# Banded attention turns placed between the half units of the query and output projections

## The chip, the cores and the metric

One NeuronCore of a Trainium2 chip runs the whole program in one launch. The metric is the device time of that core in microseconds (us). Five engines work side by side and meet only at semaphores: PE (TensorE, matrix products into PSUM banks), DVE (VectorE), ACT (ScalarE), POOL (GpSimd), and SP, whose queue issues the DMAs that bring the weights. PEld is PE's weight load.

## The reference, cut to what matters

The program is two transformer blocks, on 512 tokens of width 1024. The change lies in the second layer of the first block. That layer does, with `h` the residual stream:

```
q   = partial_rope(rmsnorm(h) @ w_q)          # 16 heads of 64; k, v: 4 shared heads, made just before
s   = q k^T / 8, masked to a band             # blocks of 128 queries x 256 keys (the block before and its own)
m   = max(max(s), sink);  e = exp(s - m)
o   = (e / (sum(e) + exp(sink - m))) @ v      # the first block of queries has no block before: its 128 keys are masked
h   = h + o @ w_o
h   = h + relu(rmsnorm(h) @ w_up)^2 @ w_down  # the MLP
h   = h + sigmoid(rmsnorm(h) @ w_gate) * (p @ w_ple_proj)
```

The last product, `p @ w_ple_proj` (the PLE product), needs nothing of `h`.

## The kernel before, in words

Activations lie transposed in SBUF: 128 features on the partitions, 512 tokens along a row, 8 such tiles for the width of 1024. The precision is that of fp32, made of three faster products: each weight and each activation is split in a high part (`w_hi`, `x0h`, `x1h`) and a rest (`w_lo`, `x0l`, `x1l`), and each 128x128x512 product is three matmuls (hi x hi, hi x lo, lo x hi).

The weights are 289 units of 512 KB, in the order in which they are used; a unit is 8 blocks of 128x128, thus 24 matmuls. They go through a ring of 4 places. SP loads unit u+4 into its place when unit u is done (`unit_done`). ACT then makes `w_hi` (`act_split`, L195), and DVE `w_lo` (`dve_split`, L203), 3 units ahead of PE. `w_lo` lies over the loaded weights. A unit's result lies in one of four banks until DVE has taken it (`bank_free`).

The order of every engine's work is the order in which the code is written; there is no planner. Around the change the stages follow each other:

- `q_*`: 8 units of `w_q`. DVE scales each result (L1169) and rotates it (L1107, L1109, L1110) with one fp32 product of PE between (`ropeswap`, L1103).
- `att_*`: 16 turns, one for each of 4 key heads and 4 blocks of queries, 4 query heads in each. A turn has four scores products (PE L1234); mask and scale on the way out of PSUM (DVE L1269, twice), maximum (L1271), three tiny ones (L1275 to L1277); four exponentials with their sums (ACT L1311) and one of the sink (L1312); the reciprocal (DVE L1282, L1283) and the scaling of the weights (L1285); 8 transposes (PE L1243), two copies (ACT L1318), four products with v (PE L1254), and the split of the output in `x1h` (ACT L1322) and `x1l` (DVE L1289). The turns overlap each other: in step T, scores of turn T stand beside transposes of T-3 and outputs of T-4. POOL copies keys, queries and values for each key head first (L1216, L1217, L1219).
- `wo_*`: 8 units of `w_o`. DVE adds each result to `h` (L1337), ACT and DVE make the MLP's input of it (`act_x` L213, `dve_x` L218), and POOL squares it and adds it up for the norm (L232, L234).
- `p_*`: the PLE product, 2 units of weights with 4 products each, kept by ACT (L1003).
- `pe_norm` (L238): PE sums POOL's squares over the partitions. The MLP follows. The scale `R` is first needed when its first result is taken.

Of the kernel before, what the change touches and what calls it, by code (L numbers as in the profile page):

```python
# [47 lines left out]
U_KV, U_Q, U_O, U_P1, U_MLP1, U_GATE1 = 90, 94, 102, 110, 112, 176  # L48
# [44 lines left out]
def program(nc, a):  # L93
    ctx = ExitStack()
    with ctx:
# [801 lines left out]
        def mlp_parts(i, n, p_in, p_out, gain):  # L897
# [99 lines left out]
        def p_scalar(e, i):  # L997
            up = (U_P0, U_P1)[i]
            for j in range(2):
                act_split(e, up + j + AHEAD, 0)  # L1000
                for mm in range(4):
                    e.wait_ge(p_mm, 8 * i + 4 * j + mm + 1)
                    e.activation(Pp[:, 4 * j + mm], bk[4 + mm], ACT.Copy).then_inc(p_out, 1)  # L1003

        def p_vector(e, i):
            up = (U_P0, U_P1)[i]
            for j in range(2):
                dve_split(e, up + j + AHEAD, 0)
                e.wait_ge(unit_done, up + j + 1)
                e.sem_inc(bank_free, 1)  # L1010

        def p_tensor(e, i):
            up = (U_P0, U_P1)[i]
            e.wait_ge(p_ready, i + 1)
            for j in range(2):
                w = (up + j) % RING
                e.wait_ge(w_split, up + j + 1)
                for mm in range(4):
                    t = 8 * i + 4 * j + mm
                    if j:  # L1020
                        e.wait_ge(p_out, t - 3)
                    for k in range(2):
                        kk = 2 * mm + k
                        e.matmul(bk[4 + mm], w_hi[:, w, kk], p_h[:, k], start=(k == 0), stop=False)
                        e.matmul(bk[4 + mm], w_hi[:, w, kk], p_l[:, k], start=False, stop=False)
                        last = e.matmul(bk[4 + mm], w_lo[:, w, kk], p_h[:, k], start=False, stop=(k == 1))
                    last.then_inc(p_mm, 1)
                e.wait_ge(p_mm, 8 * i + 4 * j + 4)
                e.sem_inc(unit_done, 1)
            e.wait_ge(p_out, 8 * i + 5)  # L1030
# [58 lines left out]
        at = [x0_at]  # L1089
        Ks = own_buf("Ks", [2, LANES + TOK])  # L1090
        Qs = own_buf("Qs", [2, 2, TOK])
        Vs = own_buf("Vs", [2, 5, 64])
        Sm = own_buf("Sm", [4, 2, 2, 256])
        PT = put("PT", [LANES, 2, 512], at=acc_at)
        st = {n: own_buf("st_" + n, [4, 4]) for n in "mx nm df sm es rc".split()}
        assert at[0] <= x0_at + 32768
# [3 lines left out]
        def rope_tensor(e, u0, j, n4, src, turn):  # L1100
            e.wait_ge(bank_free, after(u0, j, n4, 5))
            e.wait_ge(rope_steps.sem, rope_steps.at("sin", (turn[0], turn[1] - 2)))
            e.matmul(bk[5 + j % 2], C("ropeswap"), src, start=True, stop=True).then_inc(rope_mm, 1)  # L1103

        def rope_vector(e, src, j, turn):

            rope_steps.next(e, turn).took("cos", e.tensor_tensor(one(t32[:, :]), src, one(C("rcos")), ALU.mult))  # L1107
            e.wait_ge(rope_mm, turn + 1 if isinstance(turn, int) else turn[0] + (turn[1] + 1))
            rope_steps.next(e, turn).took("sin", e.tensor_tensor(a32[:, :], bk[5 + j % 2], C("rsin"), ALU.mult))  # L1109
# [23 lines left out]
        def kv_vector(e):  # L1133
            rope_steps.open(e)
            for j in range(4):
# [5 lines left out]
                if j >= 2:  # L1141
                    e.wait_ge(bank_free, U_KV + j + 3)
                    rope_vector(e, kv32[:, j - 2:j - 1], j - 2, j - 2)
# [17 lines left out]
        def q_scalar(e):  # L1161
            turns(e, 8, lambda t, j: act_split(e, U_Q + j + AHEAD, t), once=lambda: v_keep(e))

        def q_vector(e):
            def body(t, j):
                dve_split(e, U_Q + j + AHEAD, t)
                m = t * 4 + j
                b = evac_start(e, U_Q, j, t)
                e.tensor_tensor(tile(q32, m), one(b), one(R[:, :]), ALU.mult).then_inc(bank_free, 1)  # L1169
                if j:  # L1170
                    e.wait_ge(bank_free, after(U_Q, j - 1, t, 5))
                    rope_vector(e, tile(q32, t * 4 + (j - 1)), j - 1, (t * 4, j + 1))
                if j == 3:
                    e.wait_ge(bank_free, after(U_Q, j, t, 5))
                    rope_vector(e, tile(q32, m), j, (t * 4, j + 2))
            turns(e, 8, body)

        def q_tensor(e):
            def body(t, j):
                pe_unit(e, U_Q, j, t, x0h, x0l, ready(x_ready, 32) if j == 0 else None)  # L1180
                m = t * 4 + j
                if j:
                    rope_tensor(e, U_Q, j - 1, t, tile(q32, t * 4 + (j - 1)), (t * 4, j + 1))
                if j == 3:
                    rope_tensor(e, U_Q, 3, t, tile(q32, m), (t * 4, j + 2))
            turns(e, 8, body, once=lambda: v_turn(e))

        att_copied = Steps(sem("att_copies"), "K Q V")
# [4 lines left out]
        att_turned = Steps(sem("att_turned"), "t0 t1", ahead=8)  # L1196
        att_kept = Steps(sem("att_weights"), "w0 w1", ahead=8)
# [3 lines left out]
        pads = sem("pads")  # L1201
        ATT_TURNS = 16

        def att_pool(e):
            att_copied.open(e)
            e.wait_ge(unit_done, U_O)
            for t, cut in ((Ks, Ks[:, :, 0:LANES]), (Vs, Vs[:, :, 0])):
                e.memset(cut, 0.0).then_inc(pads, 1)
            e.wait_ge(rope_steps.sem, rope_steps.at("sum", 9))
            e.wait_ge(k_dup, 8)  # L1210
            e.wait_ge(kv_tok, 2)
            with e.Fori(0, 2) as i:
                for x in range(2):
                    kh = (i * 2, x)
                    e.wait_ge(att_scored.sem, att_scored.at("s", (i * 8, 4 * x - 5)))
                    att_copied.next(e, kh).took("K", e.tensor_copy(Ks[:, x:x + 1, LANES:], tile(kdup, i * 2 + x)))  # L1216
                    att_copied.next(e, kh).took("Q", e.tensor_copy(Qs[:, x], q32[:, bass.ds(i * 4 + 2 * x, 2)]))  # L1217
                    e.wait_ge(att_outputs.sem, att_outputs.at("o", (i * 8, 4 * x - 5)))
                    att_copied.next(e, kh).took("V", e.tensor_copy(Vs[:, x, 1:5], v_tok[:, :, bass.ds(i * 128 + 64 * x, 64)]))  # L1219

        def att_tensor(e):
            for s in (att_scored, att_turned, att_outputs):
                s.open(e)
            e.wait_ge(pads, 2)

            def step(i, T):
                if runs(i, T, ATT_TURNS):
                    x, n, b = T // 4, T % 4, 2 * (T % 2)
                    if n == 0:
                        e.wait_ge(att_copied.sem, att_copied.at("Q", (i * 2, x)))  # L1230
                    e.wait_ge(att_maxima.sem, att_maxima.at("m1", (i * 8, T - 2)))
                    for g in range(4):
                        hf, gg = g % 2, g // 2
                        last = e.matmul(bank[b + hf][:, gg * 256:gg * 256 + 256], Qs[64 * hf:64 * hf + 64, x, gg, n * LANES:(n + 1) * LANES],  # L1234
                                        Ks[64 * hf:64 * hf + 64, x, n * LANES:(n + 2) * LANES], start=True, stop=True)
                    att_scored.took("s", last)
                q = T - 3
                if runs(i, q, ATT_TURNS):
                    e.wait_ge(att_scales.sem, att_scales.at("scale", (i * 8, q)))
                    for kt in range(2):  # L1240
                        e.wait_ge(att_kept.sem, att_kept.at(f"w{kt}", (i * 8, q - 1)))
                        for g in range(4):
                            last = e.transpose(bank[5 + kt][:, g * LANES:(g + 1) * LANES], Sm[:, q % 4, g // 2, g % 2, kt * LANES:(kt + 1) * LANES], C("ident"))  # L1243
                        att_turned.took(f"t{kt}", last)
                q = T - 4
                if runs(i, q, ATT_TURNS):
                    x, n = q % 8 // 4, q % 4
                    if n == 0:
                        e.wait_ge(att_copied.sem, att_copied.at("V", (i * 2, q // 4)))
                    e.wait_ge(att_kept.sem, att_kept.at("w1", (i * 8, q)))  # L1250
# [1362 lines left out]
```

## Time and profile before

| | |
|---|---|
| runs, us | 2079.78, 2080.70, 2086.28; median 2080.7 |
| profiled execution, us | 2082.57 |
| its span, us | 2080.8 |
| PE busy | 1947.3 us (94%) |
| DVE busy | 1268.3 us (61%) |
| ACT busy | 900.5 us (43%) |
| POOL busy | 430.1 us (21%) |
| mean granted clock of PE | 0.975 of full speed |

A matmul counts as busy from its start to its modelled end, though the next one starts before that end; so the distance between starts, not the mean of one, says what a stream of matmuls takes. The page cuts the span into 40 slices of 52 us. PE is 90% busy or more in nearly all of them; the slices from 728 to 832 us show 60 to 70%, and next to no DMA.

### The profile page before, as it was taken

What the parts mean: (1) busy time and instruction counts of PE and PEld (TensorE: products, weight loads), DVE (VectorE), ACT (ScalarE), POOL (GpSimd) and SP (SyncE); (2) the same over time, 40 slices, a digit from 0 to 9 for tenths busy, and PEclk for the clock granted to TensorE, in tenths of its full rate; (3) what the DMA queues carried; (4) which work ended last, traced back from release to release, by engine and by line L of the source; (5) the groups of instructions that cost most, each with busy time, mean ns of one, the idle gap of its engine ahead of it and who ended that gap; (6) DMA issues with size and microseconds to landing.
All of it is one profiled execution on the core that took longest, in us unless ns stands there. A gap on an engine that the chain in (4) does not pass through costs nothing.

```text
span 2080.8 us, 27316 instructions
## 1 busy us (share of the span) xinstructions
PE 1947.3 (94%) x9494; PEld 1565.4 (75%) x9494; DVE 1268.3 (61%) x1783; ACT 900.5 (43%) x1507; POOL 430.1 (21%) x295
## 2 busy tenths in 40 slices
PE   3889999999999967999999999999999998999996
PEld 1668788888887745788888887878878886777774
DVE  7873443343469587543343468987667765777764
ACT  3674432232334255432332333445445552366661
POOL 5672200000043010300000043342212224000003
PEclk8899999999999979999999999999999999999998
DMA  4113332333332200333333332222222222212221
GB/s 178 44 34 111 91 101 91 101 92 100 95 98 90 83 1 11 92 101 93 98 97 95 101 91 81 82 61 67 66 81 64 69 72 62 90 61 63 69 72 61
DMA packets 54522, 166.98 MB, mean 80 GB/s; under 512 B 13216, under 2 KB 13344, under 8 KB 53920
## 3 DMA queue, kind: packets, MB, share of 16 engines
q1 hardware_dynamic: 54432, 165.78, 26.6%
q8 instruction: 56, 0.92, 0.2%
q14 instruction: 34, 0.28, 0.0%
HBM read 161.30 MB, written 2.10 MB: 79 GB/s over the span
## 4 chain that ended last, share of the span: by engine, by line
PE 76%; DVE 9%; ACT 5%; POOL 3%; issue 2%; DMA 2%; DVEq 0%; POOLq 0%; SPq 0%; PEldq 0%; ACTq 0%
PE bank L183 15%; PE bank L184 15%; PE bank L185 15%; PE bank L1501 4%; PE bank L1502 4%; PE bank L1503 4%; PE bank L2107 2%; DMA raw<-in_w_dram 2%; PE bank L2109 2%; PE bank L2108 2%; PE bank L1516 1%; POOL acc L234 1%; PE bank L1517 1%; PE bank L1518 1%; ACT w_hi L195 1%
## 5 line engine op out<-in xcount | busy, mean ns | idle before, releaser
L203 DVE TENSOR_TENSOR w_lo<-raw,w_hi 128x1024 fp32r<-128x1024 f32 x286 | 366.8, 1282 | 466.2 <-ACT w_hi L195 465.0
L195 ACT ACTIVATE w_hi<-raw 128x1024 fp32r<-128x1024 f32 x289 | 305.8, 1058 | 627.3 <-DMA raw<-in_w_dram 627.2
L183 PE MATMUL bank<-x1h,w_hi 128*128 128x512 f32 x744 | 291.6, 392 | 6.5 <-DVE x1l L218 6.5
L185 PE MATMUL bank<-x1h,w_lo 128*128 128x512 f32 x744 | 289.8, 389 | 0.0
L184 PE MATMUL bank<-x1l,w_hi 128*128 128x512 f32 x744 | 289.7, 389 | 0.0
L183 PE MATMUL bank<-x0h,w_hi 128*128 128x512 f32 x704 | 277.9, 395 | 0.0
L185 PE MATMUL bank<-x0h,w_lo 128*128 128x512 f32 x704 | 274.1, 389 | 0.0
L184 PE MATMUL bank<-x0l,w_hi 128*128 128x512 f32 x704 | 274.0, 389 | 0.0
L232 POOL TENSOR_TENSOR sq<-h 128x512 f32 (+1 forms) x64 | 79.0, 1234 | 783.2 <-DVEq L940 659.7
L183 PEld LDWEIGHTS bank<-x1h,w_hi 128*128 128x128 f32 x744 | 139.7, 188 | 38.0 <-DVE x1l L218 7.8
L184 PEld LDWEIGHTS bank<-x1l,w_hi 128*128 128x128 f32 x744 | 139.8, 188 | 29.3 <-issue 0.7
L185 PEld LDWEIGHTS bank<-x1h,w_lo 128*128 128x128 f32 x744 | 139.8, 188 | 29.1
L1501 PE MATMUL bank<-x1h,w_hi 128*128 128x512 f32 x384 | 156.0, 406 | 0.0
L183 PEld LDWEIGHTS bank<-x0h,w_hi 128*128 128x128 f32 x704 | 132.1, 188 | 29.8 <-issue 2.5
L184 PEld LDWEIGHTS bank<-x0l,w_hi 128*128 128x128 f32 x704 | 132.1, 188 | 29.3 <-issue 2.3
L185 PEld LDWEIGHTS bank<-x0h,w_lo 128*128 128x128 f32 x704 | 132.1, 188 | 27.5
L1502 PE MATMUL bank<-x1l,w_hi 128*128 128x512 f32 x384 | 151.1, 394 | 0.0
L1503 PE MATMUL bank<-x1h,w_lo 128*128 128x512 f32 x384 | 150.9, 393 | 0.0
L234 POOL TENSOR_TENSOR acc<-acc,sq 128x512 f32<-128x512 f32 x64 | 103.3, 1614 | 5.0
L919 DVE TENSOR_TENSOR x1l<-a,x1h 128x512 f32 x64 | 44.3, 693 | 92.7 <-ACT a L909 92.7
L907 ACT ACTIVATE x1h<-t 128x512 f32 x64 | 40.5, 632 | 130.7 <-DVE t L917 130.7
L1501 PEld LDWEIGHTS bank<-x1h,w_hi 128*128 128x128 f32 x384 | 73.0, 190 | 17.9 <-issue 1.9
(382 smaller groups left out, 3457.3 us busy)
## 6 DMA issues: line engine op xcount, KB each, us to landing
raw<-in_w_dram SPq DMA_DIRECT2D x289, 512.0 KB, 3.6
h<-in_xT_dram SPq DMA_DIRECT2D x1, 2048.0 KB, 13.0
Ur<-in_xu_dram SPq DMA_DIRECT2D x8, 256.0 KB, 2.7
out_dram<-h SPq DMA_DIRECT2D x8, 256.0 KB, 2.2
const<-in_const_dram SPq DMA_DIRECT2D x1, 1028.0 KB, 13.9
B_st<-in_B_dram SPq DMA_DIRECT2D x1, 1024.0 KB, 7.7
C_st<-in_C_dram SPq DMA_DIRECT2D x1, 1024.0 KB, 15.1
p_in<-in_pT_dram SPq DMA_DIRECT2D x1, 1024.0 KB, 4.8
```

What stands on the lines that cost most here:

```text
L183: e.matmul(b, w_hi[:, w, k], xh[:, k], start=(k == 0), stop=False)
L184: e.matmul(b, w_hi[:, w, k], xl[:, k], start=False, stop=False)
L185: last = e.matmul(b, w_lo[:, w, k], xh[:, k], start=False, stop=(k == KT - 1))
L195: e.activation(w_hi[:, z], raw[:, z], ACT.Copy).then_inc(hi_split, 1)
L203: e.tensor_tensor(w_lo[:, z], raw[:, z], w_hi[:, z].bitcast(F32), ALU.subtract).then_inc(w_split, 1)
L232: e.tensor_tensor(one(sq[:, :]), tile(h, m), tile(h, m), ALU.mult).then_inc(squared, 1)
L234: e.tensor_tensor(acc[:, :], acc[:, :], sq[:, :], ALU.add).then_inc(acc_ready, 1)
L919: e.tensor_tensor(tile(x1l, m), one(a32[:, :]), tile(x1h, m).bitcast(F32), ALU.subtract).then_inc(a_ready, 1)
L1501: e.matmul(b, w_hi[:, w, k], x1h[:, k], start=(k == 0), stop=False)
L1502: e.matmul(b, w_hi[:, w, k], x1l[:, k], start=False, stop=False)
L1503: last = e.matmul(b, w_lo[:, w, k], x1h[:, k], start=False, stop=(k == KT - 1))
L2107: e.matmul(b, w_hi[:, w, k], xh[:, k], start=(k == 0), stop=False)
```

## The change

- The stages `q_*`, `att_*` and `wo_*` and the PLE product of this layer become one window, `win_*`, of 18 places of one unit each: 8 of `w_q`, 4 of the first half of `w_o`, 2 of the PLE product, 4 of the second half of `w_o`. Each is cut in two half units of 12 matmuls, so there are 36 positions p = 0 to 35.
- `w_o` is cut by rows: the first four units use only the heads 0 to 7 for all 8 output tiles, and the last four the heads 8 to 15. Each half unit makes one output tile's half sum, and DVE adds it to `h`, so there are 16 such additions in place of 8. The two banks 0 and 1 (2 and 3 for the last unit) take the results in turn.
- Turn T of attention has its scores at position T+5, its exponentials at T+6, scaling and transposes at T+7, products with v at T+8 and the rest at T+8 and T+9. PE's order within a position is: half unit, rotation product, products with v, transposes, scores. There is now one pair of banks for the scores (2 and 3), not two, so that scores of T+1 wait for DVE's reading of T.
- The copies by POOL are gone: PE reads `kdup`, `q32` and `v_tok` themselves. In every fourth turn (first block of queries) the 128 masked keys are left out everywhere.
- The PLE product uses two banks in place of four. It no longer stands between the last unit of `w_o` and `pe_norm`.

```diff
+        Q_SLOTS, O_AT, P_AT, WIN_SLOTS = 8, (8, 14), 12, 18
+        FIRST_TURN, ATT_TURNS = 5, 16
+        def p_bank(t):
+            return bk[4 + t % 4] if t < 8 else bk[2 + t % 2]
+        def o_acc(part, i, o):
+            return bk[(2 if part and i == 3 else 0) + o]
+        def win_tensor(e):
+            for p in range(2 * WIN_SLOTS):
+                n, half = p // 2, p % 2
+                win_half(e, n, half)
...
+                if half == 0 and 1 <= n <= Q_SLOTS:
+                    e.wait_ge(bank_free, win_evacuated(n - 1))
+                    e.matmul(q_bank(n - 1), C("ropeswap"), q32[:, n - 1], start=True, stop=True).then_inc(rope_mm, 1)
+                T = turn_at(p - 3)
...
+                    e.wait_ge(att_kept.sem, att_kept.at("w", T))
...
+                T = turn_at(p - 2)
+                if T is not None:
+                    e.wait_ge(att_scales.sem, att_scales.at("scale", T))
...
+                T = turn_at(p)
...
+                    e.wait_ge(att_maxima.sem, att_maxima.at("m1", T - 1))
...
+            e.wait_ge(wo_half_free, 7)
...
+                else:
+                    e.wait_ge(wo_half_free, 4 * part + i)
...
-            att_pool(e)
...
-            q_tensor(e)
-            att_tensor(e)
-            wo_tensor(e)
+            win_tensor(e)
...
-    cols(w_o[0], 8)
+    pairs(w_o[0], 0)
     ple(w_ple_proj[1])
+    pairs(w_o[0], 1)
```

PE, in the middle of attention. `Ks`, `Qs` are keys and queries, `Sm` the weights, `PT` their transposes, `Vs` the values; each row is one group. Before:

```order
1364 L1243 MATMUL bank<-const,Sm 128x128 x8
1365 L1254 MATMUL bank<-PT,Vs 64x256 x4
1366 L1234 MATMUL bank<-Ks,Qs 128x256 x4
1367 L1243 MATMUL bank<-const,Sm 128x128 x8
1368 L1254 MATMUL bank<-PT,Vs 64x256 x4
1369 L1234 MATMUL bank<-Ks,Qs 128x256 x4
```

PE, in position 14 of the window: the end of its half unit, then (L1267) the rotation product of the unit before, and one group each of three turns. After:

```order
1368 L1219 MATMUL bank<-x0h,w_hi 128x512
1369 L1220 MATMUL bank<-x0l,w_hi 128x512
1370 L1221 MATMUL bank<-x0h,w_lo 128x512
1371 L1267 MATMUL bank<-q_124,const 128x512
1372 L1278 MATMUL bank<-PT,v_tok 64x256 x4
1373 L1287 MATMUL bank<-const,Sm_135 128x128 x8
1374 L1298 MATMUL bank<-kdup,q_124 128x256 x4
1375 L1219 MATMUL bank<-x0h,w_hi 128x512
1376 L1220 MATMUL bank<-x0l,w_hi 128x512
```

The same groups stand between half units, and the products with v have moved ahead of the transposes.

DVE, one whole step of attention before:

```order
537 L1269 SCALAR_TENSOR_TENSOR Sm<-bank,const 128x512 x2
538 L1271 TENSOR_REDUCE st_mx<-Sm 128x4
539 L1275 TENSOR_TENSOR st_mx<-st_mx,par 128x4
540 L1276 TENSOR_SCALAR st_nm<-st_mx 128x4
541 L1277 TENSOR_TENSOR st_df<-par,st_mx 128x4
542 L1282 TENSOR_TENSOR st_rc<-st_sm,st_es 128x4
543 L1283 RECIPROCAL st_rc<-st_rc 128x4
544 L1285 TENSOR_TENSOR Sm<-Sm,st_rc 128x1024
545 L1289 TENSOR_TENSOR x1l<-bank,x1h 128x2x128
```

DVE, one position with a rotation in it after, up to the next wait for scores (L1363). `q` is the query projection, `t` a temporary:

```order
522 L1319 TENSOR_TENSOR st_rc<-st_sm,st_es 128x4
523 L1320 RECIPROCAL st_rc<-st_rc 128x4
524 L1322 TENSOR_TENSOR Sm_127<-Sm_127,st_rc 128x1024
525 L1326 TENSOR_TENSOR q_124<-bank,R 128x512
526 L1108 TENSOR_TENSOR t_63<-q_124,const 128x512
527 L1346 TENSOR_TENSOR x1l<-bank,x1h 128x2x128
528 L203 TENSOR_TENSOR w_lo<-raw,w_hi 128x1024
529 L1363 SCALAR_TENSOR_TENSOR Sm_135<-bank,const 128x512 x2
530 L1365 TENSOR_REDUCE st_mx<-Sm_135 128x4
```

The scaling of q, a part of its rotation and the weight split now stand between a turn's scaling and the next turn's scores.

PE, at the end of the window. Before, a PLE product stood ahead of the norm's product (L238):

```order
1556 L1024 MATMUL bank<-p_h,w_hi 128x512
1557 L1025 MATMUL bank<-p_l,w_hi 128x512
1558 L1026 MATMUL bank<-p_h,w_lo 128x512
1559 L238 MATMUL bank<-acc,const 128x512
1560 L970 UNCONDITIONAL_BRANCH
```

After, the last half unit of `w_o` stands there:

```order
1648 L1241 MATMUL bank<-x1h,w_hi 128x512
1649 L1242 MATMUL bank<-x1l,w_hi 128x512
1650 L1243 MATMUL bank<-x1h,w_lo 128x512
1651 L238 MATMUL bank<-acc,const 128x512
1652 L973 UNCONDITIONAL_BRANCH
```

The 48 PLE matmuls that stood between `w_o` and the norm are now ahead of the last four units of `w_o`.

## Rows read from the trace of the kernel before

**Rows 1.** Busy time by stage: stretch, its length, PE, PEld, DVE, ACT, POOL, PEclk, DMA, GB/s

```profile
673.00:727.00 54.00, 53.16 (x219) 39.93 (x217) 31.04 (x41) 14.50 (x17) 0.45 (x2) 1.00 0.28 82
727.00:732.00 5.00, 0.00 (x0) 0.00 (x0) 2.66 (x4) 0.00 (x0) 1.64 (x2) 0.88 0.15 61
732.00:764.00 32.00, 22.23 (x120) 14.79 (x120) 27.67 (x58) 18.28 (x66) 4.14 (x7) 0.70 0.00 1
764.00:821.00 57.00, 39.84 (x265) 24.80 (x266) 49.62 (x102) 36.72 (x127) 2.49 (x4) 0.91 0.00 1
821.00:865.00 44.00, 44.00 (x195) 36.39 (x195) 23.56 (x24) 14.64 (x17) 19.25 (x15) 1.00 0.28 84
```

**Rows 2.** Waits of PE in 735 to 815: total, times, longest

```profile
PE bank L1243 <- DVE Sm L1285: 23.0, 13, 5.8
```

**Rows 3.** Timeline of one attention turn: start, duration, what [idle before]

```profile
776.07 1.09 PE L1243 MATMUL bank<-const,Sm 128*128 128x128 f32 x8 [0.18 <-DVE Sm L1285]
776.27 1.28 DVE L1269 SCALAR_TENSOR_TENSOR Sm<-bank,const 128x512 f32<-128x512 f32 x2
...
777.09 1.09 PE L1254 MATMUL bank<-PT,Vs 128*64 128x256 f32 x8
...
778.11 1.13 PE L1234 MATMUL bank<-Ks,Qs 64*128 64x256 f32 x8
...
779.32 0.16 DVE L1282 TENSOR_TENSOR st_rc<-st_sm,st_es 128x4 f32<-128x4 f32 x1
...
780.87 0.42 DVE L1289 TENSOR_TENSOR x1l<-bank,x1h 128x256 fp32r<-128x256 f32 x1
...
781.20 1.28 DVE L1269 SCALAR_TENSOR_TENSOR Sm<-bank,const 128x512 f32<-128x512 f32 x2
```

**Rows 4.** Timeline around two units of the query projection and its first one

```profile
673.46 0.80 PE L183 MATMUL bank<-x0h,w_hi 128*128 128x512 f32 x1
...
718.50 0.69 DVE L1169 TENSOR_TENSOR q<-bank,R 128x512 f32 x1 [0.51 <-PE bank L185]
...
722.16 1.06 ACT L195 ACTIVATE w_hi<-raw 128x1024 fp32r<-128x1024 f32 x1 [5.42 <-DMA raw<-in_w_dram]
...
724.29 0.40 PE L185 MATMUL bank<-x0h,w_lo 128*128 128x512 f32 x1
...
724.84 0.69 DVE L1169 TENSOR_TENSOR q<-bank,R 128x512 f32 x1 [0.36 <-PE bank L185]
```

**Rows 5.** Timeline from the last output unit to the norm

```profile
864.39 0.39 PE L1024 MATMUL bank<-p_h,w_hi 128*128 128x512 f32 x1
...
868.47 1.06 ACT L195 ACTIVATE w_hi<-raw 128x1024 fp32r<-128x1024 f32 x1 [1.89 <-DMA raw<-in_w_dram]
869.43 2.04 ACT L1003 ACTIVATE Pp<-bank 128x512 f32<-128x512 f32 x4
...
876.59 1.10 PE L238 MATMUL bank<-acc,const 128*128 128x512 f32 x2 [0.30 <-ACT Pp L1003]
```

**Rows 6.** Timeline of POOL and DVE where they meet, and where they don't

```profile
628.22 1.62 POOL L234 TENSOR_TENSOR acc<-acc,sq 128x512 f32<-128x512 f32 x1
628.61 1.78 DVE L1059 TENSOR_TENSOR a<-gs,Pp 128x512 f32<-128x512 f32 x1
...
650.32 0.68 DVE L1059 TENSOR_TENSOR a<-gs,Pp 128x512 f32<-128x512 f32 x1
...
838.92 1.04 POOL L232 TENSOR_TENSOR sq<-h 128x512 f32 x1 [2.81 <-DVEq L1339]
840.04 1.62 POOL L234 TENSOR_TENSOR acc<-acc,sq 128x512 f32<-128x512 f32 x1
```

**Rows 7.** Stage table around an idle stretch of PE elsewhere

```profile
1734.00:1738.00 4.00, 0.00 (x0) 0.00 (x0) 2.36 (x3) 3.16 (x4) 2.49 (x2) 0.97 0.30 118
1738.00:1742.00 4.00, 2.65 (x6) 2.17 (x7) 2.83 (x4) 0.00 (x0) 0.00 (x0) 0.50 0.00 0
1742.00:1746.00 4.00, 4.00 (x14) 3.14 (x13) 0.00 (x0) 0.00 (x0) 0.00 (x0) 0.68 0.00 0
```

More of the change, by code:

```diff
@@ L1200, in program @@
         att_lo = Steps(sem("att_out_lo"), "lo", ahead=8)
[L1201 to L1219, printed above, removed]
@@ L1236, in step @@
                     att_scored.took("s", last)
[L1237 to L1250, printed above, removed]
-                    e.wait_ge(att_lo.sem, att_lo.at("lo", (i * 8, q - 2)))
-                    for hf in range(2):
-                        for kt in range(2):
-                            last = e.matmul(bank[7 - 3 * (q % 2)][64 * hf:64 * hf + 64, 0:256], Vs[:, x, n + kt], PT[:, kt, hf * 256:hf * 256 + 256], start=(kt == 0), stop=(kt == 1))
-                    att_outputs.took("o", last)
@@ L1301, in att_scalar, with win_scalar @@
+        def win_scalar(e):
             for s in (att_exps, att_kept, att_hi):
                 s.open(e)
-            def step(i, T):
-                q = T - 1
-                if runs(i, q, ATT_TURNS):
-                    z = q % 4
-                    e.wait_ge(att_maxima.sem, att_maxima.at("dif", (i * 8, q)))
+            for p in range(2 * WIN_SLOTS + 1):
+                n, half = p // 2, p % 2
+                T = turn_at(p - 1)
+                if T is not None:
+                    z, k0 = T % 4, keys(T)
+                    e.wait_ge(att_maxima.sem, att_maxima.at("dif", T))
@@ L1332, in wo_vector @@
-        def wo_vector(e):
-            def body(t, j):
-                dve_split(e, U_O + j + AHEAD, t)
-                m = t * 4 + j
-                b = evac_start(e, U_O, j, t)
-                e.tensor_tensor(tile(h, m), tile(h, m), one(b), ALU.add).then_inc(bank_free, 1)
-                e.wait_ge(bank_free, after(U_O, j, t, 5))
-                e.sem_inc(h_ready, 1)
-                dve_x(e, 5, m, "mlp1", x0h, x0l)
-            turns(e, 8, body, late=lambda: p_split_vector(e, 1))
-        def wo_tensor(e):
-            def there(k):
-                return att_lo.sem, att_lo.at("lo", 4 * (k // 2) + 3)
-            turns(e, 8, lambda t, j: pe_unit(e, U_O, j, t, x1h, x1l, there if j == 0 else None))
+                if half == 0 and n < WIN_SLOTS:
+                    act_split(e, U_Q + n + AHEAD, 0)
@@ L2505, in cols, with pairs @@
             unit(w, r0, c0 + 128 * m)
+    def pairs(w, pair):
+        w = w[pair * 512:pair * 512 + 512].reshape(4, 128, 4, 2, 128)
+        for j in range(4):
+            units.append(w[:, :, j].transpose(1, 2, 0, 3).reshape(128, KT, 128))
     def ple(w):
```

361 lines of the change are left out of this document (220 added, 141 removed).

## The prediction

> **What bounds the kernel now.** I read the page's slices first, then the table by stage, then the waits and the timeline of one turn. PE is the bound nearly everywhere. Two stretches differ [rows 1]: 727 to 732, where PE does nothing, and 732 to 821, where PE's overlapping records cover 62 of 89 us. There DVE is busy 77.3 of 89 us, and 49.6 of 57 from 764 on. PE's waits in that stage name DVE's scaling of the weights [rows 2]. One turn shows the same [rows 3]: DVE starts the masks at 776.27 and again at 781.20, so a turn takes 4.93 us, and DVE has no gap in it. PE's three groups start at 776.07, 777.09 and 778.11, some 3.1 us of work, and then PE waits. So 16 turns with start and end cost the 94 us from 727 to 821 [rows 1], of which PE has about 50 us of work at full clock (16x3.1).
>
> The stretch that the change rewrites runs from the first product with `w_q`, at 673.5, to the norm's product, at 876.6 [rows 4, 5]. That is **203.1 us** before.
>
> **Is it hidden?** The total of PE's work in the new window is easily summed. Twelve matmuls at the distance of 0.2265 us of the stream (24 of them and one rotation product of 0.87 give the 6.34 us from 718.50 to 724.84 [rows 4]) are 2.72 us a half unit, and 32 of these are 87. The rotations add 7, the PLE products 11.2, v's transposes 1, and attention 43 (3.06 for each of 12 full turns, about 1.6 for each of 4 short ones). That is 149 us, and 54 us could go. But DVE's work doesn't shrink, and PE and DVE now wait for each other once in each position. So I add up the chain, not the work.
>
> Call S the moment at which the scores of a position are ready. Durations are those of rows 3 and 4:
>
> - DVE: masks 1.31, maximum 1.25, three tiny ones 0.5: 3.06 from 776.27 to 779.32 with no gap. Then reciprocal and scaling of the turn before, 1.55 (779.32 to 780.87). So scaled weights are there at S+4.7.
> - An even position with a rotation: DVE takes q next, 0.61 and 0.1 to be seen, at S+5.45. PE's half unit ended at S+2.7 and its rotation product waits for that. Behind it are queued products with v, transposes and scores: 0.87+3x1.02. The period is **9.4 us**, of which PE waits 2.7.
> - An odd position: PE waits with the transposes for S+4.75, then 2x1.02 and 0.13: **6.9 us**. DVE has as much of its own: 4.6, half of the rotation 1.45, rest of the output 0.36, new masks.
>
> The short turns have no row. The nearest are the 512 and the 256 elements of DVE, 0.68 and 0.42. I take 0.75 for the masks, 0.65 for the maximum, 0.6 for scaling, and half for PE and ACT. Then every cycle of four positions is 8.2 + 5.8 + 8.9 + 6.85 us. Were the cut worth nothing, the window would be 12 us longer; that is the upper bound, and I take the lower, since time follows size in the two rows.
>
> | positions | us |
> |---|---|
> | 0 to 4: five halves 13.6, two rotations 1.7, v's transposes 1.0, one wait of 0.7 | 17.0 |
> | 5, first scores behind the rotation's sum | 4.05 |
> | 6, 7: pipeline fills | 11.6 |
> | 8 to 16: 3x8.9 + 2x8.2 + 2x6.85 + 2x5.8 | 68.4 |
> | 17: its half unit writes the bank of the last rotation, and waits for DVE to read it: 5.5+2.72+2x1.02+0.6 | 10.9 |
> | 18 to 20: 5.8 + 5.85 + 7.2 (DVE also splits `p`) | 18.9 |
> | 21 to 23: last turns | 15.1 |
> | 24 to 27: PLE | 16.2 |
> | 28 to 35: last four units | 26.4 |
> | wait for the norm | 8.0 |
> | sum | **196.5** |
>
> The last three need words. **PLE:** with two banks the third product waits until ACT has kept the first. ACT's queue has the split of a weight unit in front of that, and this waits for a DMA. From the end of a unit to ACT's start took 3.7 to 4 us (864.3 to 868.47 [rows 5]; 718.2 to 722.16 [rows 4]). So PE waits about 2 us in each unit, beside 11.2 of work and 0.7 at the ends. Before, four banks hid the same thing but for 0.3 us at each end.
>
> **Last four units:** bank 0 is written by every unit's first half, and only DVE's addition frees it. DVE's queue has in front of it the weight split, which waits for ACT, which waits for the DMA: 3.95+1.05+1.2, then `x0l` 0.7 and the addition 0.7 behind the end of the unit before. That is 7.6 and more, against 5.44: about 1.2 us in each unit and 0.2 for the second bank. 4x5.44 + 4.6 = 26.4.
>
> **Norm:** before, 12.2 us of PLE product (864.4 to 876.6) covered POOL's last squares. Now nothing does. POOL's two operations for a tile take 2.66 plus 0.1 [rows 6], and tiles come every 3 to 4 us. Rows 6 also show that POOL and DVE block each other: DVE's product of two SBUF tensors took 1.78 us where it began inside POOL's addition, 0.68 where POOL was idle. DVE has the split and two `x0l` in each unit. POOL's 2x2.45 (what is left of 2.66 once blocked parts go) and DVE's 2.4 make 7.3 us a unit, more than the 6.6 in which tiles come. POOL thus ends some 8 us behind PE: 3.7 for DVE's last addition and the last tile, the rest in arrears. Without any blocking it would be about 6, with full blocking and dearer additions 9.5.
>
> The Trainium skill (SBUF — State Buffer, section SBUF: two separate sides) says that VectorE and GpSimd share one pair of ports under an exclusive lock that the first holds for its whole instruction. The trace agrees: 0.39 us after POOL's start, DVE's operation lasted until 0.55 us behind POOL's end.
>
> **Clock.** After a stretch in which PE was idle (1734 to 1738), the granted clock was 0.50 and 0.68 for the next 8 us [rows 7]: 4x0.5+4x0.32 = 3.3 us lost, part of it still idle. The wait for the norm is 8 us long, so I add **2.2** (bounds 0 and 3.3). In exchange the half clock of the old attention stage (0.70 from 732 to 764) goes; it cost little there, as DVE set the pace.
>
> So 196.5+2.2 = 198.7 against 203.1: **4.4 us less**. The profiled execution took 2082.57 (span 2080.8 and 1.8 around it), 1.9 above the median of 2080.7; the same span with 4.4 less is 2078.2, and against the median of the runs it is **2076.3**, say 2076.
>
> Costed at nothing: POOL's copies (PE's idle stretch from 727 to 732, which goes with them, is inside the 94); the eight further additions to `h` (0.61 each, in positions 17 to 24 beside PE's chain, in the end inside the 26.4); the changed order of weights (same bytes); the missing loops. ACT was busy for 55 us in the old stage's 89 [rows 1], 3.4 a turn; with half a weight split that is 4 us in a position, beside 5.8 or more.
>
> **Rivals.**
>
> *A. The waits overlap better than my chain* (DVE's reading released earlier, fewer serial steps). For it: PE's work is only 149 us. Against: every link of the chain stands in one queue behind the other. If half of the 27 us that I count as waits for DVE in positions 6 to 17 went, the time would be 2063.
>
> *B. Slower: PE's clock falls inside the window.* Place: positions 6 to 23, where PE waits 1.5 to 2.7 us in each. In the old stage it had 0.70 and 0.91 [rows 1] with waits of much that size. At half clock a position takes 11 us for 6.9 and 13.5 for 9.4, about 4.1 more; over 16 positions 66 us. The share at which it decides is 7%: then the 4.4 us are gone. At one fifth, 13 us, the time is 2089. Against it: PE will be at work for 75 to 80% of the time there, against 62 of 89 with smaller products, and half units at the full array stand between.
>
> The Trainium skill (TensorE: Matmul & The Clock Gate, section A second HAM failure mode: psum-queue depth-cycling) says that short idle times between groups of matmuls can make the clock swing. The trace agrees for the old stage, with 0.70 and 0.91; whether it holds with the half units in between, no row shows.
>
> *C. The steps between engines are dearer than the rows.* Each position has five waits of PE that were not there. At 0.1 us more in each, over 36 positions, 4 us: the change brings nothing, 2080.
>
> *D. The change hides nothing of attention.* Then only short turns and POOL's copies count, with the end's 8 us against them: also about 2080. It would need positions of 8.7 us on average from 6 to 23, against my 6.9.
>
> **Chances.** Forecast 0.38, of which half lies beyond 0.3% (6.2 us, about what a measurement of this kernel can tell) and half within. A 0.23. B 0.21. C and D together 0.18. So faster 0.19+0.23 = 0.42, same 0.19+0.18 = 0.37, slower 0.21. The forecast's own range is 2070 to 2081. The range to hold 8 in 10 goes down to A with half of its gain and half again as much, 2062, and up to B's 2089 and a little, 2090.
>
> **What would show it.** Right: in the new profile from the first `w_q` product to L238 some 198 us; a distance of 9 us between the scores (L1298) of an odd and the next even position, and under 7 for the other; PE's longest single wait at L238, 6 to 10 us, released by POOL; two waits of 2 us at the PLE products for ACT. Wrong: a granted clock under 0.95 over the window (B), distances of 8 and 6 (A), or 10 and 8 (C); a wait at L238 under 4 us, if POOL keeps up. The rest of the program must take the same time, but for a shift.

## The result and the profile after

| | before | after |
|---|---|---|
| runs, us | 2082.15 median of 7 (2077.93 to 2086.28) | 2094.4 median of 7 (2091.95 to 2100.59) |
| ratio, 95% interval | | 1.0069 [1.0051, 1.0086] |
| span of the profiled execution, us | 2080.8 | 2092.6 |
| PE busy, us | 1947.3 (94%) | 1947.2 (93%) |
| mean granted clock | 0.975 | 0.976 |
| first product with `w_q` to L238, us | 203.1 | 209.9 (670.16 to 880.02) |

The changed kernel is slower by 12 us by the medians (14 by the ratio), and the forecast of 2076 was wrong, in sign too. PE's busy time is the same to 0.1 us, which doesn't say where the time went: a wait is not busy, a slow clock makes the same work longer, and the short turns took work away. So I read the rewritten stretch by stages, which answers to [rows 1]. Columns: stretch, length, PE, PEld, DVE, ACT, POOL, granted clock, DMA share, GB/s.

```profile
691.00:764.00 73.00, 60.36 (x330) 39.76 (x332) 58.97 (x118) 34.77 (x115) 0.00 (x0) 1.00 0.13 40
764.00:778.00 14.00, 9.14 (x36) 5.35 (x34) 7.98 (x15) 4.59 (x17) 0.00 (x0) 0.76 0.05 20
778.00:792.00 14.00, 8.52 (x38) 5.73 (x34) 6.80 (x13) 3.50 (x12) 0.00 (x0) 0.76 0.08 17
792.00:811.00 19.00, 17.18 (x102) 11.92 (x104) 17.19 (x35) 11.72 (x37) 0.00 (x0) 1.00 0.14 45
811.00:827.00 16.00, 14.66 (x85) 10.33 (x84) 11.98 (x21) 7.51 (x21) 0.00 (x0) 1.00 0.12 34
827.00:844.00 17.00, 13.14 (x48) 9.19 (x47) 2.87 (x3) 6.18 (x11) 0.00 (x0) 0.92 0.20 62
844.00:872.00 28.00, 23.23 (x96) 17.83 (x96) 14.78 (x15) 8.88 (x11) 17.49 (x13) 0.99 0.24 76
872.00:880.00 8.00, 0.00 (x0) 0.01 (x1) 5.06 (x6) 2.79 (x4) 5.25 (x4) 0.71 0.21 66
880.00:887.00 7.00, 6.98 (x17) 4.88 (x18) 3.71 (x2) 1.63 (x2) 0.53 (x1) 0.60 0.00 0
```

Attention no longer leaves PE at 62 of 89 us: through 691 to 764 PE is busy for 60.4 of 73 us at full clock. The stretches that stand out are two of 14 us from 764 to 792, with the clock at 0.76, and the 8 us from 872 to 880, where PE does nothing, with 0.60 behind them. PE's waits from 673 to 900 (what waits, the releaser, total us, times, longest) name all three places:

```profile
PE bank L238 <- POOL acc L234: 8.7, 1, 8.7
PE bank L1287 <- DVE Sm L1322: 7.7, 8, 2.3
PE bank L1267 <- DVE q L1326: 7.6, 4, 2.4
PE bank L1241 <- DVE a L1113: 5.5, 1, 5.5
PE bank L1241 <- DVE x1l L1346: 4.9, 1, 4.9
PE bank L1013 <- ACT Pp L1005: 3.5, 2, 2.1
PE bank L1241 <- DVE h L1336: 3.4, 2, 2.7
```

The 23.0 us for the scaled weights [rows 2] are now 7.7. In their place stand four waits for q's reading (L1267), one for a rotation (L1113), one for the norm, and the wait for `x1l`, 4.9 us, which my table didn't have. Its place in the timeline, position 16, the first half unit of `w_o`:

```profile
764.84 1.29 DVE L1363 SCALAR_TENSOR_TENSOR Sm<-bank,const 128x512 f32<-128x512 f32 x2 [0.16 <-PE bank L1298]
...
768.30 1.22 DVE L1322 TENSOR_TENSOR Sm<-Sm,st_rc 128x1024 f32<-128x1024 f32 x1
769.44 0.68 DVE L1326 TENSOR_TENSOR q<-bank,R 128x512 f32<-128x512 f32 x1
770.16 0.69 DVE L1108 TENSOR_TENSOR t<-q,const 128x512 f32<-128x512 f32 x1
770.77 0.42 DVE L1346 TENSOR_TENSOR x1l<-bank,x1h 128x256 fp32r<-128x256 f32 x1
...
771.24 0.80 PE L1241 MATMUL bank<-x1h,w_hi 128*128 128x512 f32 x1 [4.86 <-DVE x1l L1346]
771.84 0.63 PE L1242 MATMUL bank<-x1l,w_hi 128*128 128x512 f32 x1
...
784.31 0.77 PE L1241 MATMUL bank<-x1h,w_hi 128*128 128x512 f32 x1 [5.48 <-DVE a L1113]
```

PE stops in the middle of the half unit: it needs the output of turn 7 (heads 4 to 7), and DVE makes the low part of that output only behind this position's masks, scaling, q and cosine. The matmuls behind it show the clock: 0.63 us for 0.39, and starts 0.43 us apart for 0.23. The clock had already fallen inside the wait: it was at half from 769.6 to 776.4, while the wait ended at 771.2. The end, which answers to [rows 5] and [rows 6]:

```profile
870.39 1.06 ACT L195 ACTIVATE w_hi<-raw 128x1024 fp32r<-128x1024 f32 x1 [4.29 <-DMA raw<-in_w_dram]
871.48 1.23 DVE L203 TENSOR_TENSOR w_lo<-raw,w_hi 128x1024 fp32r<-128x1024 f32 x1 [3.29 <-ACT w_hi L195]
...
873.29 0.68 DVE L1336 TENSOR_TENSOR h<-h,bank 128x512 f32<-128x512 f32 x1
874.28 1.04 POOL L232 TENSOR_TENSOR sq<-h 128x512 f32 x1 [2.95 <-DVEq L1339]
875.40 1.59 POOL L234 TENSOR_TENSOR acc<-acc,sq 128x512 f32<-128x512 f32 x1
877.17 1.04 POOL L232 TENSOR_TENSOR sq<-h 128x512 f32 x1 [0.18 <-POOL acc L234]
878.29 1.59 POOL L234 TENSOR_TENSOR acc<-acc,sq 128x512 f32<-128x512 f32 x1
```

L238 starts behind the last of these, at 880.02, after 8.74 us of wait. POOL was not behind when this wait began. It stood idle for 2.95 us until DVE had added the seventh tile to `h` (873.29), and DVE's queue had a weight split ahead of that addition, which waited for ACT, which waited for a DMA. The rest, 5.6 us, is POOL's work for the last two tiles.

### The profile page after: what moved, and what is told of

The parts are those of the page before. It is cut to its first block, busy times and chain, and to the rows that moved or that the text cites. A ratio compares the mean times of both kernels' runs of the same rounds, so it can differ in the third digit from the quotient of the medians.

```text
span 2092.6 us, 27161 instructions
## 1 busy us (share of the span) xinstructions
PE 1947.2 (93%) x9462; PEld 1557.9 (74%) x9462; DVE 1263.3 (60%) x1791; ACT 896.9 (43%) x1503; POOL 421.9 (20%) x281
## 4 chain that ended last, share of the span: by engine, by line
PE 74%; DVE 10%; ACT 6%; DMA 3%; issue 3%; POOL 2%; DVEq 0%; POOLq 0%; SPq 0%; PEldq 0%
PE bank L183 14%; PE bank L185 13%; PE bank L184 13%; PE bank L1561 4%; PE bank L1563 3%; PE bank L1562 3%; DMA raw<-in_w_dram 3%; PE bank L2167 2%; PE bank L2169 2%; PE bank L2168 2%; PE bank L1576 1%; ACT w_hi L195 1%; PE bank L1577 1%; PE bank L1578 1%; DVE w_lo L203 1%
## 5 line engine op out<-in xcount | busy, mean ns | idle before, releaser
L183 PE MATMUL bank<-x1h,w_hi 128*128 128x512 f32 x680 | 266.6, 392 | 6.4 <-DVE x1l L218 6.4
L185 PE MATMUL bank<-x1h,w_lo 128*128 128x512 f32 x680 | 264.9, 390 | 0.0
L184 PE MATMUL bank<-x1l,w_hi 128*128 128x512 f32 x680 | 264.8, 389 | 0.0
L183 PE MATMUL bank<-x0h,w_hi 128*128 128x512 f32 x640 | 251.6, 393 | 0.0
L184 PE MATMUL bank<-x0l,w_hi 128*128 128x512 f32 x640 | 249.7, 390 | 0.0
L185 PE MATMUL bank<-x0h,w_lo 128*128 128x512 f32 x640 | 249.7, 390 | 0.0
L1561 PE MATMUL bank<-x1h,w_hi 128*128 128x512 f32 x384 | 156.6, 408 | 0.0
L1563 PE MATMUL bank<-x1h,w_lo 128*128 128x512 f32 x384 | 151.8, 395 | 0.0
L1562 PE MATMUL bank<-x1l,w_hi 128*128 128x512 f32 x384 | 151.8, 395 | 0.0
L184 PEld LDWEIGHTS bank<-x1l,w_hi 128*128 128x128 f32 x680 | 127.8, 188 | 27.0 <-issue 0.7
L185 PEld LDWEIGHTS bank<-x1h,w_lo 128*128 128x128 f32 x680 | 127.8, 188 | 26.6
L184 PEld LDWEIGHTS bank<-x0l,w_hi 128*128 128x128 f32 x640 | 120.6, 188 | 26.2 <-issue 1.2
L185 PEld LDWEIGHTS bank<-x0h,w_lo 128*128 128x128 f32 x640 | 120.6, 188 | 25.2
```

The lines of the kernel that those rows point to most:

```text
L183: e.matmul(b, w_hi[:, w, k], xh[:, k], start=(k == 0), stop=False)
L184: e.matmul(b, w_hi[:, w, k], xl[:, k], start=False, stop=False)
L185: last = e.matmul(b, w_lo[:, w, k], xh[:, k], start=False, stop=(k == KT - 1))
L1561: e.matmul(b, w_hi[:, w, k], x1h[:, k], start=(k == 0), stop=False)
L1562: e.matmul(b, w_hi[:, w, k], x1l[:, k], start=False, stop=False)
L1563: last = e.matmul(b, w_lo[:, w, k], x1h[:, k], start=False, stop=(k == KT - 1))
```

## The experiments

Theories. **T1**: the wait for turn 7 and the clock behind the two 5 us waits make the miss. **T2**: positions are dearer than the chain throughout, so the interleaving doesn't pay. **T3**: the end (PLE ahead, norm bare) makes it. Each run stands as its ratio to runs of before on its own chip, whose medians were 2080.1 to 2081.9. "Window" is the stretch from the first `w_q` product to L238 in the profiled execution; in after it is 209.9, and the distances between scores are 9.2, 7.3, 8.1 and 6.0 in a cycle of four, 14.0 in position 16 and 14.2 in 17.

**1. No wait for turn 7.** The first half unit reads heads 0 to 3 twice; the second takes the wait.

```diff
+                    early = n == O_AT[0] and half == 0
-                        e.wait_ge(att_lo.sem, att_lo.at("lo", 8 * part + 4 * (k // 2) + 3))
-                    x = 4 * part + k
+                        e.wait_ge(att_lo.sem, att_lo.at("lo", 3 if early else 8 * part + 4 * (k // 2) + 3))
+                    x = 4 * part + (k % 2 if early else k)
```

> Changes part of the computation: the first half unit of the output projection (position 16) reads the head tiles 0 and 1 twice, in place of 2 and 3, so that it need not wait for turn 7's output, which DVE makes in the same position. All else as in the changed kernel. Theory 1 (the missed wait and the clock that falls behind it): the 4.86 us wait goes, position 16 takes 9 us in place of 14.0 from scores to scores, no half clock begins there; 5 us less in the window, 210 to 205, and if the next wait (position 17, 5.5 us) alone is too short to lower the clock, 3 more. Rival 2 (every position is dearer than counted, the waits only show it): the wait moves to the next position, window 208 or more.

Measured: 2087.5, ratio 1.0028 [1.0011, 1.0046]. Position 16 takes 9.2 for 14.0. Position 17 takes 13.1; in its stretch the clock is still down. The window is 207.8, 2.1 less where I expected 5: two ordinary positions took 1.6 and 0.5 more than in after, since the clock fell there too, and it fell once more in the last four units (at 856.4). That is not rival 2, since the wait of position 17 did not grow (5.4 us for 5.5).

```profile
764.00:778.00 14.00, 9.13 (x54) 5.47 (x48) 11.84 (x21) 7.43 (x24) 0.00 (x0) 1.00 0.14 39
778.00:792.00 14.00, 10.67 (x54) 7.86 (x56) 7.94 (x20) 4.90 (x19) 0.00 (x0) 0.76 0.11 37
```

So this wait is a cause, 4.8 us with its clock, and it is not the whole of the 12.

**2. Matmuls into both waits.** 18 and 17 products of 128x512 into banks that are overwritten before they are read; the waits for DVE stay.

```diff
+                if n == O_AT[0] and half:
+                    e.wait_ge(att_kept.sem, att_kept.at("w", 9))
+                    filler(e, 17, w, bk[4])
...
+                if n == O_AT[0] and half == 0:
+                    e.wait_ge(att_lo.sem, att_lo.at("lo", 3))
+                    filler(e, 18, w, bk[0])
```

> Adds 18 matmuls of 128x128x512 ahead of the half unit of position 16 and 17 ahead of that of position 17, into banks that are free then; their results are overwritten, and the output is the same. They fill some 4 us of each of the two waits, which end when they did. Theory 1 (the clock falls because PE idles for 5 us): no half clock from 760 to 800; the positions take 11.3 and 10.9 us in place of 14.0 and 14.2, window 6 us shorter, 204. Rival 2 (the clock falls for another reason, as the small products of attention): the half clock stays, and the window is as long or longer (18 matmuls at half clock are 7.7 us).

Measured: 2085.0, ratio 1.0008 [0.9991, 1.0024]. Positions 16 and 17 take 11.6 each. The window is 207.2, 2.7 less, where I expected 204; the profiled execution, 2092.1 us, was the second longest of its ten.

```profile
694.00:704.00 10.00, 8.63 (x37) 6.17 (x38) 7.11 (x14) 2.72 (x11) 0.00 (x0) 0.83 0.16 53
...
710.00:716.00 6.00, 3.55 (x11) 1.47 (x11) 5.49 (x10) 3.12 (x10) 0.00 (x0) 0.84 0.00 0
...
770.00:782.00 12.00, 11.21 (x56) 7.80 (x56) 8.45 (x16) 4.98 (x19) 0.00 (x0) 1.00 0.10 38
782.00:794.00 12.00, 10.68 (x61) 7.66 (x59) 6.80 (x13) 4.05 (x13) 0.00 (x0) 1.00 0.11 31
```

More work for PE made the kernel faster, so the clock behind the waits costs by itself: 28.2 - 23.2 = 5.0 us in the two positions. The first two rows show the same execution with a lower clock in two ordinary places where after had 1.00. Such falls come and go between executions, and the medians of this section contain them.

**3. Matmuls ahead of the norm.** 68 products of 128x256 into a free half of a bank.

```diff
+        def filler(e, count, w):
+            for _ in range(count):
+                e.matmul(bank[6][:, 256:512], w_hi[:, w, 0], x1h[:, 0, 0:256], start=True, stop=True)
...
+            filler(e, 68, 3)
```

> Adds 68 matmuls of 128x128x256 ahead of the norm's product, into a bank that is free; output the same. They fill 7.7 of the 8.7 us in which PE waits for POOL. Theory 1: the wait's end doesn't move, the clock stays full behind it, and from the norm's product to the third result of the MLP it takes 18 us as before the change, not 20.5: 2.5 us less in all. Rival 2 (what comes behind the norm is late for DVE's or ACT's sake): nothing changes there.

Measured: 2090.4, ratio 1.0032 [1.0015, 1.0049]; window 209.7. L238 now takes 1.10 us for 2.04, and behind it the clock stays up:

```profile
870.00:878.00 8.00, 8.00 (x68) 7.84 (x66) 5.48 (x6) 3.17 (x4) 5.00 (x4) 1.00 0.22 66
878.00:886.00 8.00, 7.58 (x33) 5.93 (x32) 5.18 (x3) 1.63 (x2) 0.84 (x2) 1.00 0.01 2
```

From L238 to the third result of the MLP it takes 17.9 us for 20.5, so the clock behind the norm costs 2.6 us in the profiles; I had 2.2. The medians differ by 4.0, with intervals that nearly touch.

**4. PLE product last**, with its four banks, in the interleaved order.

```diff
-            return bk[4 + t % 4] if t < 8 else bk[2 + t % 2]
+            return bk[4 + t % 4]
-        Q_SLOTS, O_AT, P_AT, WIN_SLOTS = 8, (8, 14), 12, 18
+        Q_SLOTS, O_AT, P_AT, WIN_SLOTS = 8, (8, 12), 16, 18
...
-                    e.wait_ge(p_out, t - 1)
+                    e.wait_ge(p_out, t - 3)
```

> Undoes one part: the PLE product stands again behind the last unit of the output projection, with four banks. Theory 1: PE's wait of 8.7 us at the norm goes, and the two waits of 2 us for ACT at the PLE products shrink to 0.3; the third cost, bank 0 waiting for DVE in the last four units, stays; the clock behind the norm stays full (2.6). In all 12 to 14 us less, window 197, the total equal to the kernel before or slightly under. Rival 2 (POOL is so far behind that the 12 us of PLE don't cover it, or the second half of the output projection now waits for turn 15's output): 5 us less at most.

Measured: 2075.4, ratio 0.9966 [0.9947, 0.9986]; window 195.7, 14.2 less, and no half clock behind the norm.

```profile
PE bank L1241 <- DVE a L1113: 5.5, 1, 5.5
PE bank L1241 <- DVE x1l L1347: 4.9, 1, 4.9
PE bank L1241 <- DVE h L1337: 2.7, 1, 2.7
...
PE bank L238 <- ACT Pp L1005: 0.3, 1, 0.3
PE bank L1013 <- ACT Pp L1005: 0.3, 1, 0.3
```

The largest single cost of the change is the PLE product's new place, together with its two banks for four, which this run doesn't separate: 19 us by the medians. T3 holds as a price. But my sum had 12.0 of the 14.2 us of window.

**5. Four banks for the last units**, so that PE need not wait for DVE's additions.

```diff
-            return bk[(2 if part and i == 3 else 0) + o]
+            return bk[(2 if part and i % 2 else 0) + o]
...
```

> One change against the changed kernel: the last four units of the output projection go over four banks in place of two. Same output. Theory 1: PE's waits for DVE's additions there (3.4 us in all) go, and so does most of the gap between the units; but the norm's product still waits for POOL, which gets each tile only when DVE comes to it; so PE just waits longer at the norm (8.7 to 11) and the window is within 1 us of 209.9. Rival 2 (the banks hold the whole tail back): window 3 us shorter or more.

Measured: 2091.8, ratio 1.0048 [1.0031, 1.0065], not told apart from after. Window 212.0, of which two ordinary positions have a lower clock. The waits for additions are gone, and the norm's took their place:

```profile
PE bank L238 <- POOL acc L234: 12.1, 1, 12.1
PE bank L1013 <- ACT Pp L1005: 2.8, 1, 2.8
```

PE reached the norm earlier and L238 came no sooner. Here POOL does run behind: its last four tiles follow each other with 0.18 us between tiles, up to 882.8, where in after it stood idle for 2.95 us and then had two tiles left. So with the end as it is, DVE's and POOL's queues set L238, and a faster PE only waits longer.

**6. DVE takes q first.** In even positions DVE reads the bank of `w_q` (L1326) ahead of the reciprocal and the scaling, not behind them. Same instructions, other order.

```diff
+                m = n - 1
+                if half == 0 and 0 <= m < Q_SLOTS:
+                    e.wait_ge(unit_done, U_Q + m + 1)
+                    e.tensor_tensor(q32[:, m], q_bank(m), R[:, :], ALU.mult).then_inc(bank_free, 1)
```

> One change of order on DVE against the changed kernel: in even positions it takes q out of its bank before the scaling of the turn before, not behind it. Same instructions. Theory 1 (a chain through one queue sets the length of a position): the rotation product starts 1.5 us earlier, PE then waits for the scaling for a part of that; even positions take 8 us in place of 9.2, others are unchanged; window 5 to 6 us shorter, 204. Rival 2 (DVE is simply full and order doesn't matter): no position changes by more than 0.3 us.

Measured: 2084.4, ratio 1.0025 [1.0015, 1.0034]; window 203.1, 6.8 less. Positions of 9.2 take 7.6, those of 8.1 take 6.6. The four waits of 7.6 us in all become two:

```profile
PE bank L1241 <- DVE a L1113: 5.5, 1, 5.5
PE bank L1241 <- DVE x1l L1347: 4.7, 1, 4.7
...
PE bank L1267 <- DVE q L1318: 1.8, 2, 0.9
```

**7. The joint reordered.** In position 16 DVE makes turn 7's low part first, in position 17 the last rotation first.

```diff
+                if p == 16:
+                    rest()
+                if p == 17:
+                    rope_sin(e, q32[:, 7:8], q_bank(7), 9)
```

> Two changes of order on DVE, in positions 16 and 17 alone: turn 7's output (for which PE waits 4.9 us) is made ahead of the scaling in 16, and the last rotation (5.5 us of wait) ahead of it in 17. Theory 1: the waits shrink to 2 and 4 us and the positions to 11.5 and 10.5 with a full clock, 12 to 13 if one half clock remains; window 4 to 9 us shorter. Rival 2 (the clock falls for the attention products): waits shrink, but half clock stays at 770 to 795 and the gain is under 4 us.

Measured: 2090.5 of four runs, ratio 1.0055 [1.0034, 1.0075], unclear by the runs. In the trace the window is 204.3; the positions take 10.6 and 11.6, with waits of 2.0 and 3.9 us, and at each the clock is down for less long:

```profile
763.50:774.50 11.00, 9.01 (x38) 4.87 (x38) 8.45 (x16) 5.08 (x19) 0.00 (x0) 0.84 0.10 39
774.50:786.00 11.50, 7.56 (x38) 5.27 (x36) 6.80 (x13) 3.51 (x13) 0.00 (x0) 0.85 0.10 19
```

Two slow stretches of 3.4 us where after had two of 6.8.

**8. The kernel before with short turns and direct reads alone**: no POOL copies, 128 masked keys left out of every fourth turn, no interleaving. The turns are written out in place of a loop, as in after.

```diff
+        def keys(T):
+            return 128 if T % 4 == 0 else 0
...
-            att_pool(e)
```

> The kernel before, with one part of the change alone: no copies by POOL (PE reads keys, queries and values themselves) and 128 keys in place of 256 in every fourth turn. Nothing is interleaved. Theory 1 (the interleaving itself, with the waits it makes, costs more than it hides): DVE sets the pace of the old stage, 4.93 us a turn; four turns lose 1.7 each, 6.9, and the start loses its 4.4 us for the copies. 11 us less than the kernel before, 2071, so that of the changed kernel's result the interleaving has cost some 20. Rival 2 (the short turns save little, for DVE's fixed costs): 5 us less at most, 2077.

Measured: 2074.5, ratio 0.9969 [0.9957, 0.9980]; window 193.1, 10 less than before's, where I expected 11. The medians differ by only 6 where I expected 10. A short turn's operations took 0.76, 0.69 and 0.69 us on DVE, where I had put 0.75, 0.65 and 0.6.

**9. Full turns in the window.** The first block of queries attends to 256 keys, the first 128 repeated; its result is another one.

```diff
-            return 128 if T % 4 == 0 else 0
+            return 0
```

> The changed kernel without the short turns: every fourth turn reads 256 keys as the others do (for the first block of queries those of blocks 0 and 1 under the ordinary mask, so its result is another). Theory 1: 12 us more by my chain (8.2 becomes 9.4 and so on), window 222; the interleaving by itself then stands at 2106 against 2081, and what held the changed kernel near the one before was the part that has nothing to do with interleaving. Rival 2 (positions are bound by PE's own work): 6 us more at most.

Measured: 2105.9, ratio 1.0113 [1.0087, 1.0139]; window 221.3, 11.4 more than after.

**10. All repairs** (4, 5, 6 and 7 together). Edit: the lines of those four.

> The changed kernel with all repairs: PLE product last, on four banks; four banks for the last four units of the output projection; q taken first in even positions; the two changes of order in 16 and 17. Same computation. Theory 1: from the window of 195.7 us with PLE last, 5.6 go for the even positions, 4 to 9 for positions 16 and 17, 3 for the banks: 178 to 183, total 2058 to 2063, under the kernel before by 1%. Rival 2 (the savings overlap, since each only moves PE's wait to the next link): 190 or more, 2070.

Measured: 2062.2, ratio 0.9904 [0.9890, 0.9919]; window 181.9. Positions 16 and 17 take 11.0 and 11.6, with waits of 2.6 and 3.9 us and a granted clock of 0.84 and 0.85 over them.

**11. All repairs, and 8 and 11 matmuls into the two waits that are left.**

```diff
+                    filler(e, 11, w, bk[4])
...
+                    filler(e, 8, w, bk[0])
```

> The kernel with all repairs, and 8 and 11 further matmuls of 128x128x512 in the two waits that are left in positions 16 and 17 (2.6 and 3.9 us); their results are overwritten. Theory 1: in the repaired kernel's profile two half clocks of 3.4 us lie there, and these positions took 11.0 and 11.6 us; with the clock held they take 9.5 to 10.5 each, 2 to 3 us less in all, total 2059. Rival 2 (the waits are too short to matter to the clock): no change, 2062.

Measured: 2054.7, ratio 0.9871 [0.9849, 0.9893]; window 176.9. Positions 16 and 17 take 9.4 and 10.0, 3.2 us less. The medians differ by 7.5 where I expected 2 to 3; in this profile the clock never falls in the window, where run 10's had one more fall, at an ordinary position (709.3).

```profile
670.00:765.00 95.00, 86.71 (x443) 59.14 (x443) 76.90 (x147) 47.05 (x139) 0.00 (x0) 1.00 0.17 51
765.00:786.00 21.00, 19.86 (x115) 13.99 (x111) 15.88 (x30) 9.98 (x29) 0.00 (x0) 1.00 0.09 26
786.00:847.00 61.00, 55.92 (x274) 42.36 (x274) 46.07 (x63) 29.44 (x63) 24.70 (x17) 1.00 0.23 69
```

This version beats both kernels, before by 1.3%; 0.3% of that is what run 8 had without interleaving.

## Why the prediction was wrong, step by step

The window was to be 196.5 and was 209.9. By places in after:

| step | predicted | measured |
|---|---|---|
| to the scores of position 7 | 32.65 | 32.4 |
| positions 8 to 15 | 59.5 | 61.1 |
| position 16 | 8.9 | 14.0 |
| position 17 | 10.9 | 14.2 |
| 18 to 20 | 18.9 | 18.9 |
| 21 to 27 | 31.3 | 33.1 |
| last four units | 26.4 | 27.4 |
| wait for the norm | 8.0 | 8.7 |
| clock behind it | 2.2 | 2.6 |

- **The step that failed** has two parts, both in positions 16 and 17: a wait that my sum left out, 2.7 us, and the clock of long waits inside the window, which I put at nothing, 5.0 us. The first is the row "8 to 16: 3x8.9 + ...": I priced position 16 as one more even position. Its half unit is the first of `w_o`, and its second half reads heads 4 to 7. The wait for `w_o`'s operand stood nowhere in my sum; I had followed banks and rotations only. At full clock it costs 11.6 - 8.9 = 2.7 (run 2), and 9.2 without it (run 1) shows that 8.9 was right for the rest.
- **The clock in the window.** Rival B named it and put it in the wrong place. It asked for 7% of positions 6 to 23 at half clock, through waits of 1.5 to 2.7 us. In after the ordinary positions from 691 to 764, with such waits, had 1.00. The falls came in the two waits of about 5 us, lasted 6.8 us each, and cost 5.0 us in all (run 2) where rival B charged 4.1 for each position hit. I had position 17's wait right, 5.5 for 5.48, and gave it no clock, although I had charged the norm's wait 2.2. The two positions are 8.4 of the 13.4 us: 3.4 from waits, 5.0 from the clock. T1 thus explains most of the miss in the window, not all. The Trainium skill (TensorE: Matmul & The Clock Gate, section A second HAM failure mode: psum-queue depth-cycling) says that frequent short idle times between groups of matmuls can make the clock swing. Some executions agree at ordinary positions, with half clock for 3.4 us at 702.8 and 740.3 in run 1; the two falls of after are another case, each at one long wait.
- **The chain per position** was right in its kind: T2 explains only 1.6 us over eight positions. That is rival C at a fifth of a microsecond each. Part of it is my distance of the stream: (6.34 - 0.87)/24 is 0.228, not 0.2265, which is 0.02 us a half unit.
- **The end** was near in size: PE's waits for ACT at the PLE product are 1.4 and 2.1 us (I had 2 and 2), the norm's wait 8.7 for 8.0, released by POOL. But its working does not give the 8.0: 7.3 for 6.6 us a unit is 2.8 over four units, and with 3.7 makes 6.5. Nor were there such arrears, since POOL stood idle for 2.95 us before its last two tiles; what I left out is DVE's weight split, which waited for the DMA ahead of the seventh tile. The 8.0 was partly luck. In the last four units 7.6 against 5.44 is 2.2 us a unit, where I wrote 1.2; measured are 27.4 for 26.4 in all. The PLE row's parts add up to 15.9, not 16.2. Run 4 puts the PLE's move at 14.2 us of window. My terms for it were 16.2 - 12.2 for the product and 8.0 for the norm, 12.0 in all; most of the rest are the 1.8 us too few in 21 to 27, where the clock was at half from 841.3 to 844.7, a fall that I hadn't charged.
- **What the sum compares with.** Before to after is a chain of three steps. Short turns and direct reads: 203.1 to 193.1 (run 8). Interleaving with the PLE last: 193.1 to 195.7. The PLE's move: 195.7 to 209.9. In ratios 0.9969, 0.9966 and 1.0069, so the middle step is nothing that the runs can tell. So the interleaving in this order, net of its own waits, brings nothing, which is what rival D said. Its 8.7 us a position does not belong to its 2080: 18 positions of 8.7 are 32 us more than my chain, and 2080 needs 4. From the scores of position 5 at 690.99 to the PLE's first product at 826.81 are 7.5 for each of 18, where I had 6.9, and that was enough. With the changes of runs 5 to 7 added (run 10) the interleaving does pay: 193.1 becomes 181.9, and 0.9969 becomes 0.9904. Without the move of the PLE my sum stood at 184.5, and 195.7 was measured.
- **Chances.** Slower had 0.21, by B alone. D with the end at my own terms (12.0 and 2.2 of clock, where I wrote 8) would have stood at 2086, 5.5 above before, just inside what I counted as the same.

From the profiled windows +6.8 and the clock +2.6 make 9.4 of the 12.2 us between the medians. The other 2.8 stay open. Outside the window the two profiles differ by 3.3 us less ahead of it and 5.8 more behind, and neither need be a cost of the change: from L238 to the end, the same code as in after took 1204.6 us in run 1 and 1206.0 in run 5, against 1212.6 in after and 1204.2 in before.

## What to carry over

When units with different operands are lined up in one queue, the ordinary cycle isn't the risk (it was right within 3%): for the first consumer of every late tile, find where the producer's queue makes that tile, and charge each long wait of PE with the clock that goes with it. Order and banks decided here whether the change paid. Runs 4 to 7 changed no arithmetic: the PLE product put back turned 1.0069 into 0.9966, and DVE's order with two more banks for the last units turned that into 0.9904. Work that stands ahead of a reduction is its cover; once it is moved away, a faster PE only waits longer.

## What the runs showed of the hardware

Single waits in otherwise steady work brought the clock down from 2.4 to 1.2 GHz. In after it was at half from 769.6 to 776.4 and from 783.2 to 790.1 us, 6.8 us each time, from 1.6 and 1.1 us before the end of the waits of 4.9 and 5.5 us. All five other profiles with both waits (runs 3, 4, 5, 6 and 9) show two such falls of 6.8 us. At waits of 2.0 to 3.9 us it was at half for 3.4 us (runs 7 and 10); with matmuls in the waits so that 0.8 to 1.1 us were left, it stayed at full speed (runs 2 and 11). The length of one wait doesn't decide alone: in after the ordinary positions, with waits of up to 2.4 us, kept the full clock. Filling idle time with useless matmuls thus paid three times: by 9, 4 and 7.5 us of the medians (runs 2, 3 and 11 against after, after and run 10).

POOL and DVE blocked each other here as in [rows 6], and POOL was held up for longer. In after, DVE's product of SBUF tensors:

```profile
851.51 0.75 DVE L218 SCALAR_TENSOR_TENSOR x0l<-h,par,x0h 128x512 fp32r<-128x512 f32 x1 [0.85 <-ACT x0h L213]
...
856.75 1.75 DVE L218 SCALAR_TENSOR_TENSOR x0l<-h,par,x0h 128x512 fp32r<-128x512 f32 x1
```

The second one ended 0.55 us after POOL's addition, which ran from 855.83 and took 2.12 us itself, against 1.29 for the one before it.
